# The end of a two-layer hybrid backbone: last down products by column halves, the other passes' sums gated on GpSimd and added by TensorE

## What is computed

```python
def moe_swiglu(h, w_router, wg, wu, wd):
    logits = (h @ w_router).astype(jnp.float32)
    top_v, top_i = lax.top_k(logits, TOP_K)
    top_w = jax.nn.softmax(top_v, axis=-1)
    gates = jnp.einsum('blk,blke->ble', top_w, jax.nn.one_hot(top_i, N_EXPERTS, dtype=jnp.float32)).astype(h.dtype)
    y = jnp.zeros_like(h)
    for e in range(N_EXPERTS):
        y = y + gates[..., e:e + 1] * swiglu(h, wg[e], wu[e], wd[e])
    return y

def post_norm(x, y, gate, g, b):
    return layer_norm(ALPHA * x + gate * y, g, b)
```

## Time and profile before

| | |
|---|---|
| runs of the kernel before | 1333.41, 1333.41 and 1337.09 us, median 1333.41 |
| the profiled execution's own time | 1337.3 us |
| its span in the profile | 1335.4 us |
| mean granted TensorE clock | 0.975 |
| last down products begin | 1301.28 us |
| combination begins on TensorE | 1314.10 us |
| last VectorE operation ends | 1332.38 us |

### The profile page before, as it was taken

The page is one execution under the profiler, slowest core; times in us unless marked ns, Lnnn a source line. Parts: engine busy times, 40 slices in busy tenths (PEclk is TensorE's granted clock), DMA queues, the critical chain, the costliest instruction groups (busy, mean ns, idle before and its releaser), DMA issues.

```text
span 1335.4 us, 17338 instructions
## 1 busy us (share of the span) xinstructions
PE 1278.3 (96%) x6503; PEld 959.3 (72%) x6504; DVE 715.0 (54%) x1026; ACT 521.6 (39%) x632; POOL 131.2 (10%) x119
## 2 busy tenths in 40 slices
PE   4999999999999989999999999999999999999994
PEld 2555449999999964677646886765467878888882
DVE  1101456334234252555335777743256788888888
ACT  0101025233233242234202746533136666777772
POOL 0420003200000033000000010100102021202020
PEclk8999999999999989899998789999999999999997
DMA  9986386424324184720405666859989899999993
GB/s 365 351 340 247 107 319 190 158 95 161 122 94 157 47 320 144 263 78 24 173 0 194 243 228 257 294 193 341 352 317 338 293 338 357 383 366 385 362 358 142
DMA packets 125356, 317.10 MB, mean 237 GB/s; under 512 B 12931, under 2 KB 47078, under 8 KB 124774
## 3 DMA queue, kind: packets, MB, share of 16 engines
q1 hardware_dynamic: 119264, 295.00, 60.7%
q0 software_dynamic: 5744, 21.07, 5.1%
q10 hardware_dynamic: 278, 0.10, 0.0%
HBM read 306.37 MB, written 9.76 MB: 237 GB/s over the span
## 4 chain that ended last, share of the span: by engine, by line
PE 89%; DVE 5%; DMA 3%; issue 1%; SPq 1%; ACT 1%; DVEq 0%; ACTq 0%
PE ps L2546 10%; PE ps L2547 10%; PE ps L2548 10%; PE ps L2244 8%; PE ps L2246 8%; PE ps L2245 8%; PE ps L2209 7%; PE ps L2552 7%; PE ps L2146 6%; PE ps L2336 3%; DMA sb_ring<-in_ev_w_in 2%; PE ps L2106 2%; PE ps L2438 1%; PE ps L2080 1%; DVE sb_expert_lo L1753 1%
## 5 line engine op out<-in xcount | busy, mean ns | idle before, releaser
L1753 DVE TENSOR_TENSOR sb_expert_lo<-sb_expert_raw,sb_expert_hi 128x1792 fp32r<-128x1792 f32 (+1 forms) x210 | 334.1, 1646 | 85.0 <-PE ps L2552 73.7
L1201 ACT CAST sb_expert_hi<-sb_expert_raw 128x1792 fp32r<-128x1792 f32 (+1 forms) x210 | 283.4, 1392 | 117.3 <-PE ps L2548 78.4
L2546 PE MATMUL ps<-sb_expert_hi,sb_expert_x 128*128 128x448 f32 x448 | 166.9, 373 | 4.5 <-DVE sb_expert_lo L1753 2.5
L2547 PE MATMUL ps<-sb_expert_lo,sb_expert_x 128*128 128x448 f32 x448 | 165.3, 369 | 0.0
L2548 PE MATMUL ps<-sb_expert_hi,sb_expert_x 128*128 128x448 f32 x448 | 165.0, 368 | 0.0
L2244 PE MATMUL ps<-sb_split_acts,sb_split_weights 128*128 128x384 f32 x352 | 118.0, 335 | 0.4 <-issue 0.4
L2246 PE MATMUL ps<-sb_split_acts,sb_split_weights 128*128 128x384 f32 x352 | 117.9, 335 | 0.0
L2245 PE MATMUL ps<-sb_split_acts,sb_split_weights 128*128 128x384 f32 x352 | 117.7, 334 | 0.0
L2546 PEld LDWEIGHTS ps<-sb_expert_hi,sb_expert_x 128*128 128x128 f32 x448 | 85.2, 190 | 20.1 <-issue 12.7
L2548 PEld LDWEIGHTS ps<-sb_expert_hi,sb_expert_x 128*128 128x128 f32 x448 | 85.0, 190 | 7.2
L2547 PEld LDWEIGHTS ps<-sb_expert_lo,sb_expert_x 128*128 128x128 f32 x448 | 85.1, 190 | 7.0
(11 more groups left out here) (339 smaller groups left out, 1835.5 us busy)
## 6 DMA issues: line engine op xcount, KB each, us to landing
sb_expert_raw<-in_moe_w_gate SPq DMA_DIRECT2D x128, 448.0 KB, 5.6
sb_expert_raw<-in_moe_w_up SPq DMA_DIRECT2D x128, 448.0 KB, 7.0
sb_expert_raw<-in_moe_w_down SPq DMA_DIRECT2D x112, 512.0 KB, 7.3
sb_ring<-in_ada_w SPq DMA_DIRECT2D x14, 3072.0 KB, 17.7
sb_ring<-in_ffn_w_gate SPq DMA_DIRECT2D x44, 256.0 KB, 3.8
sb_ring<-in_ffn_w_up SPq DMA_DIRECT2D x44, 256.0 KB, 4.7
sb_ring<-in_ffn_w_down SPq DMA_DIRECT2D x22, 512.0 KB, 6.3
sb_ring<-in_ev_w_in SPq DMA_DIRECT2D x4, 2048.0 KB, 15.4
```

The lines of the kernel that those rows point to most:

```text
L1201: nc.scalar.copy(EHI[piece.h][:, 0:w], ERAW[:, r, 0:w]).then_inc(e_hi, 1)
L1753: V.tensor_tensor(ELO[r][:, 0:w], ERAW[:, r, 0:w], EHI[piece.h][:, 0:w].bitcast(F32), ALU.subtract)\
L2546: first = mm(out, lh, rh, start=start, stop=False)
L2547: mm(out, lh, rl, start=False, stop=False)
```

## The change

- SP issues the loads of the other passes' sums right behind the last weight load; the gate rows follow, once the tokens are split. `sums_room` is gone.
- GpSimd waits for the gate rows instead of the last of the sums before it loads gain and bias, and then multiplies the sums of groups 1 and 2 by the latent gate, in place, signalling `sums_gated`.
- VectorE keeps the multiplication and the scaled addition for group 0 alone. It gates the last pass's result in four pieces of 512 columns, in place of two of 1024. In `summed`, ALPHA times x is taken for groups 1 and 2.
- TensorE makes the last down products piece by piece for both column halves up to the fourth piece; for the last three it makes all of the first half, signals, then all of the second, and signals again. The gated sums of groups 1 and 2 are added into the PSUM banks by products with the identity, one for each bank, between the products with the one-hot matrix.

```diff
--- before.py
+++ after.py
...
@@ -805,12 +805,11 @@
                 expert_down(e_last(more, b), e, EB + b)
 
             sp.wait_ge(stored, 16 * 2 * DEPTH)
-            tokens_split(sp, (more, 0), 0)
-            sp.dma_start(GB[:, :, :], gate_rows[1, 2:4, :].partition_broadcast(P)).then_inc(gates_back, 16)
-            sp.wait_ge(sums_room, 1)
             sp.wait_ge(y_stored, nth((more, 0), 16, 16 * (len(SECOND) - 1)))
             for g in range(NG):
                 sp.dma_start(YG[:, g, :], expert_sums[g * P:(g + 1) * P, :]).then_inc(y_got[g], 16)
+            tokens_split(sp, (more, 0), 0)
+            sp.dma_start(GB[:, :, :], gate_rows[1, 2:4, :].partition_broadcast(P)).then_inc(gates_back, 16)
             for g in range(NG):
                 sp.wait_ge(y_full, g + 1)
                 out = y_prompt[0] if g == 0 else y_sample[0, (g - 1) * P:g * P, :]
@@ -967,9 +966,12 @@
             with pool.Fori(0, more) as j:
                 fetch((j, 1), j * 2 + n)
                 add_rows((j, -1), j * 2 + (n + 1))
-            pool.wait_ge(y_got[NG - 1], 16)
+            pool.wait_ge(gates_back, 16)
             pool.dma_start(LG[:, :], ln_g[1, 1].partition_broadcast(P)).then_inc(lnp_in, 16)
             pool.dma_start(LB[:, :], ln_b[1, 1].partition_broadcast(P)).then_inc(lnp_in, 16)
+            for g in range(1, NG):
+                pool.wait_ge(y_got[g], 16)
+                pool.tensor_tensor(YG[:, g, :], YG[:, g, :], GB[:, 1, :], ALU.mult).then_inc(sums_gated, 1)
 
 
         @block.scalar
@@ -1995,9 +1997,8 @@
             ch.n = more * per + base
             for c in range(3):
                 expert_low(e_last(more, c), "d")
-            V.tensor_copy(ROWW[:, 2, :], ROWW[:, 1, :]).then_inc(sums_room, 1)
+            ch(V.tensor_copy(ROWW[:, 2, :], ROWW[:, 1, :]))
             expert_low(e_last(more, 3), "d")
-            dve.wait_ge(sums_room, 1)
             dve.wait_ge(disp_ps, seen((more, 0), 1))
             for g in range(NG):
                 ch(V.tensor_scalar(SM[:, 36 + g:37 + g], ROWW[:, 2, 0:1], -float(P * g), None, ALU.add))
@@ -2007,26 +2008,23 @@
                 expert_low(e_last(more, c), "d")
             dve.wait_ge(gates_back, 16)
 
-            def before_last(g):
-
-                dve.wait_ge(y_got[g], 16)
-                dve.wait_ge(x_full, NG * (2 * DEPTH - 2) + g + 1)
-                ch(V.tensor_tensor(T[:, :], YG[:, g, :], GB[:, min(g, 1), :], ALU.mult))
-                ch(V.scalar_tensor_tensor(X[:, g, :], X[:, g, :], ALPHA, T[:, :], ALU.mult, ALU.add))
-
-            before_last(0)
-            before_last(1)
-            dve.wait_ge(yd, seen((more, 0)))
-            for v in range(2):
-                V.scalar_tensor_tensor(YV[:, v, :], PS[:, 4:6, :].rearrange("p a n -> p (a n)"), ROWW[:, 2, 1:2], GB[:, v, :],
-                                       ALU.mult, ALU.mult).then_inc(y_gated, 1)
+            dve.wait_ge(y_got[0], 16)
+            dve.wait_ge(x_full, NG * (2 * DEPTH - 1))
+            ch(V.tensor_tensor(YG[:, 0, :], YG[:, 0, :], GB[:, 0, :], ALU.mult))
+            ch(V.scalar_tensor_tensor(X[:, 0, :], X[:, 0, :], ALPHA, YG[:, 0, :], ALU.mult, ALU.add))
+            for q in range(2):
+                half = slice(q * 512, (q + 1) * 512)
+                dve.wait_ge(yd, seen((more, 0)) + q)
+                for v in range(2):
+                    V.scalar_tensor_tensor(YV[:, v, half], PS[:, 4 + q, :], ROWW[:, 2, 1:2], GB[:, v, half],
+                                           ALU.mult, ALU.mult).then_inc(y_gated, 1)
 
             def summed(g):
 
                 x = X[:, g, :]
                 dve.wait_ge(comb_ps, g + 1)
                 at = (0, 2, 6)[g]
-                ch(V.scalar_tensor_tensor(x, PS[:, at:at + 2, :].rearrange("p a n -> p (a n)"), 1.0, x, ALU.mult, ALU.add,
+                ch(V.scalar_tensor_tensor(x, x, ALPHA if g else 1.0, PS[:, at:at + 2, :].rearrange("p a n -> p (a n)"), ALU.mult, ALU.add,
                                           accum_out=SM[:, 28 + g:29 + g]))
                 V.tensor_scalar(SM[:, 16 + g:17 + g], SM[:, 28 + g:29 + g], -1.0 / D, None, ALU.mult).then_inc(mean_ready, 1)
 
@@ -2040,7 +2038,6 @@
                 rsqrt(13 + g, 2 * g, 1)
                 V.scalar_tensor_tensor(x, x, SM[:, 2 * g + 1:2 * g + 2], LB[:, :], ALU.mult, ALU.add).then_inc(y_full, 1)
 
-            before_last(2)
             summed(0)
             summed(1)
             dve.wait_ge(lnp_in, 48 * (2 * DEPTH - 1) + 32)
@@ -2744,14 +2741,55 @@
             more = more_items(pe)
             with pe.Fori(0, more) as j:
                 pass_products((j, 0), (j, -1))
-            down((more, -1), 1, [e_last(more, b) for b in range(EB)], lambda: None, False)
+            LATE = 3
+
+            def last_down(p, pieces):
+
+                b = blocks_of(p)[0]
+
+                def product(j, q):
+                    cols, half, r, hi = slice(b.home(j), b.home(j) + b.n), slice(q * 512, (q + 1) * 512), pieces[j].r, pieces[j].h
+                    return three_products(PS[:, b.down[0] + q, :], (EHS[1][0][:, cols], EHS[1][1][:, cols]),
+                                          (EHI[hi][:, half], ELO[r][:, half]), False, j == EB - 1)[1]
+
+                hidden_split(pe, p, 1, 0)
+                for j in range(EB - LATE):
+                    piece_ready(pieces[j])
+                    product(j, 0)
+                    product(j, 1).then_inc(e_used, 1)
+                for j in range(EB - LATE, EB):
+                    piece_ready(pieces[j])
+                    last = product(j, 0)
+                last.then_inc(yd, 1)
+                for j in range(EB - LATE, EB):
+                    last = product(j, 1)
+                last.then_inc(yd, 1)
+
+            def sums_part(g, q):
+
+                if q == 0:
+                    pe.wait_ge(sums_gated, g)
+                mm(PS[:, (0, 2, 6)[g] + q, :], ident, YG[:, g, q * 512:(q + 1) * 512], start=True, stop=False)
+
+            def last_part(g, q):
+
+                v = min(g, 1)
+                pe.wait_ge(y_gated, 2 * q + v + 1)
+                return mm(PS[:, (0, 2, 6)[g] + q, :], OH[:, g * P:(g + 1) * P], YV[:, v, q * 512:(q + 1) * 512],
+                          start=(g == 0), stop=True)
+
+            last_down((more, -1), [e_last(more, b) for b in range(EB)])
             pe.wait_ge(one_hot_ready, 1)
-            for g in range(NG):
-                pe.wait_ge(y_gated, min(g, 1) + 1)
-                for h in range(2):
-                    last = mm(PS[:, (0, 2, 6)[g] + h, :], OH[:, g * P:(g + 1) * P], YV[:, min(g, 1), h * 512:(h + 1) * 512],
-                              start=True, stop=True)
-                last.then_inc(comb_ps, 1)
+            last_part(0, 0)
+            sums_part(1, 0)
+            last_part(0, 1).then_inc(comb_ps, 1)
+            sums_part(1, 1)
+            last_part(1, 0)
+            last_part(1, 1).then_inc(comb_ps, 1)
+            for q in range(2):
+                sums_part(2, q)
+                last = last_part(2, q)
+            last.then_inc(comb_ps, 1)
 
 
 # ---- launch: one core; inputs and outputs as the reference has them ----
```

4 lines of the change are left out of this document (2 added, 2 removed).

## The result

| | before | changed |
|---|---|---|
| median of 6 runs each | 1335.25 us (1331.60 to 1339.34) | 1343.44 us (1338.96 to 1344.01) |
| the profiled execution | 1337.3 us, span 1335.4 | 1342.03 us, span 1340.2 |
| mean granted TensorE clock | 0.975 | 0.974 |

The ratio is 1.005, 95% interval 1.0027 to 1.0073: slower by some 6.7 us (the medians lie 8.2 us apart). The middle of the interval is beyond the 0.3% that the forecast called "no change". The forecast was 1331.8 us and its range ended at 1336.5. Of the 11.6 us between forecast and measurement, 1.8 are the kernel before itself, which measured 1335.25 here and 1333.41 when the forecast was made.

The account below looks back on a forecast made before the run. TensorE, busy 96%, bounds the kernel; only the end chain could move. Group 1's addition starting 1.6 us earlier takes the profiled 1337.3 to 1335.7; 3.9 us lower on the median, 1331.8 us, range 1329.3 to 1336.5.

Parts of the forecast that it names:

- no change: Whole kernel: a difference within about 0.3%, 4.0 us, which a measurement cannot tell; chance of landing within, 0.81.
- The forecast's chain: End of the last low part to the start of group 1's addition, forecast to start 1.6 us earlier.
- The collision: VectorE and GpSimd operations with two SBUF inputs exclude each other; VectorE's addition of group 0 goes first, chance 0.38.
- T: Landing time of the gate rows, which opens VectorE's gating operations and GpSimd's work: 1308.4, range 1306.5 to 1310.1.
- GpSimd comes first: Rival: GpSimd's multiplication takes the operands before VectorE's addition of group 0, TensorE's clock falls; 1335.0 us, chance 0.27.
- Each waits for the whole of the other, in turn: Collision rule read from the feed-forward stage: VectorE's two subtractions took 6.53 us together, GpSimd's next operation 3.27.
- The clock: TensorE's combination: clock stays high, an fp32 product costing 0.86 us, not 1.71; its fall before cost 1.7 us.
- slower: Whole kernel: a time over 1337.4 us, from a part of the collisions; chance 0.07.

Follow-up runs that it names:

- filler: Changed kernel plus 25 unread products on TensorE between the last down products and the combination; median 1341.53 us.
- in turn: Changed kernel, with GpSimd's second multiplication waiting for the end of its first; median 1340.78 us.
- VectorE multiplies: Changed kernel, with VectorE doing GpSimd's multiplications of groups 1 and 2 as well; median 1336.74 us.
- gates first: Changed kernel with gate rows loaded before the sums, gating before group 0's scaled addition, GpSimd's multiplications waiting for VectorE's; median 1333.99 us, again 1335.55.
- order undone: Changed kernel with only the load order undone, gate rows ahead of the sums; median 1337.81 us.
- loads behind: Changed kernel with GpSimd's two LayerNorm loads issued behind its multiplications; one execution, 1341.12 us.

## Why the prediction was wrong, point by point

The forecast's chain was 10.5 us (12.13 - 1.6), the measured one 18.06. Step by step, from the end of the last low part:

| step | forecast | measured | off by |
|---|---|---|---|
| until VectorE's multiplication starts (gate rows) | 1.17 | 1.43 | +0.26 |
| multiplication and scaled addition | 2.50 | 7.25 | +4.75 |
| until TensorE's first combining product | 0.85 | 1.02 | +0.17 |
| from there to group 1's addition | 6.0 | 8.36 | +2.36 |

- **The step that failed is "The collision".** It had GpSimd ready at T + 1.4 and VectorE's addition at T + 1.41, 0.01 us later, and let VectorE come first without a reason. So the addition of group 0 stood in the sum at 1.22 us, and it took 5.99. GpSimd won in all four executions of this arrangement (changed twice, filler, in turn), with rows that start 0.22 to 0.23 us after VectorE's. The rival "GpSimd comes first" named the mechanism and had 0.27; it was the right one by sign.
- **Its price was half of what it is.** "Each waits for the whole of the other, in turn" was read from one meeting in the feed-forward stage, and gave the rival 2.35 us. Here it was 4.77 us, both multiplications. The prediction didn't say that GpSimd's first two rows there are parted by a wait (L851 is issued through `ch`), and in the changed kernel nothing parts the two. The run with a wait between them gives 3.69 - 1.22 = 2.47, the rival's price: so its 1335.0 us fell short by the second multiplication. The Trainium skill, page SBUF — State Buffer, section "SBUF: two separate sides", says that whichever of the two starts first gets the shared pair for the whole instruction. That the addition is held up as a whole agrees (5.99 us). Two things here differ, and the measurement decides: the row that starts first is VectorE's, by 0.23 us, and it stood behind two instructions, not one.
- **The clock.** The forecast kept it at 1.00 through an idle 0.7 us; the rival charged 1.7 us. The idle became 6.08 us, and the clock cost 2.9 us in that execution and 1.75, the rival's price, in the second, against the filler run's 5.42. Idle stretches up to 2.48 us (VectorE multiplies) left it at 1.00, those of 3.72 us and more brought it to 0.50; the kernel before lost it behind 2.87.
- **T was sized a little early**: 1308.4 forecast. VectorE's multiplication comes 1.43 us behind the low part, which in the times of the trace before is 1308.8 for the forecast's 1308.55. It is a quarter of a microsecond, inside the bounds given.
- **Right:** no stall in the last down products, (1309.08 - 1299.52) / 41 = 0.233 us apart; four gating pieces 2.73 us where 2.8 was forecast, beside GpSimd or not; the six products at the high clock 5.42 us against 5.15 and 0.2 for the release; two SBUF operands collide with GpSimd, PSUM and SBUF do not. The end behind group 1's addition is 13.21 instead of 12.9: ahead of L2036 VectorE waits 0.32 us for its own result.
- **What the parts are worth** when the collision falls on nobody: with the parts of the change ordered well ("gates first"), -3.3 us of chain, of which the halves are 1.7.

The chance of 0.07 for "slower" came from pricing every collision as one GpSimd instruction. Had the second multiplication stood in the rival, it would have read 1335.0 + 2.35 = 1337.4 us with its 0.27, and with the clock at 2.9 instead of 1.7 another 1.2, 1338.6; the range would have had to reach there. In chain this is 12.13 + 1.6 + 2.35 + 1.2 = 17.3 us, where 18.06 and 17.31 were measured.

## What to carry to other kernels

Work with SBUF operands moved to GpSimd beside a VectorE operation with two SBUF operands can hold that operation up by more than one GpSimd instruction (here by two), so price it at the sum of those that stand back to back, add the clock that TensorE's idle then costs, and give that case a range of its own even when the two seem to meet by chance. Put the operations that nobody waits for (here the scaled addition) where the collision falls, and those on the path (here the gating, with one operand in PSUM) ahead of it: one moved line gave back the whole loss. A delay of half a microsecond on GpSimd took away as much chain in one execution, but it holds no order; a wait on a semaphore does.

## What was unexpected of the hardware

- GpSimd passed with two instructions in a row against a waiting VectorE operation (5.99, 5.98 and 6.10 us for the addition), where its loads were issued right ahead of them. In the two kernels in which its first multiplication had itself been released by a transfer, the engines alternated (3.26 and 3.25 us for the addition). In the feed-forward stage they alternate as well: VectorE's second subtraction gets in between GpSimd's second and third row (the third, L851 from 228.14, takes 3.37 us), and no wait parts these two. In these three cases GpSimd's first row starts 0.30, 0.41 (order undone) and 1.20 us (loads behind) ahead of the operation that it holds up; where two pass, it starts 0.23 us behind it. Which of these differences decides isn't settled: a run with other distances between GpSimd's issues and its first multiplication was not made, and the start of a GpSimd row is rough.
- Who wins doesn't follow the rows' starts below some tenths of a microsecond: VectorE lost with a lead of 0.22, won with 0.70, and won with 0.05 where both had waited for the same landing.
- The gate rows took 7.9 to 10.1 us to land behind the 1.5 MB of the sums on the same queue (nine traces, eight of them 9.3 or more), and 6.2 to 7.7 us ahead of them (five traces, the kernel before with 7.3).
